# Expert value rows on TensorE as four 64x64 products, with no share for VectorE

## The chip, the cores and the metric

The kernel runs on one core of a Trainium2 chip. The metric is the device time of one execution in microseconds. Three executions of the kernel before took 3182.41, 3187.84 and 3185.2 us (median 3185.2 us).

## The reference, cut to what matters

The program is a transformer block with a mixture of convolution and RWKV, followed by a PEER feed-forward with 16384 experts, followed by two further layers (differential attention, then latent attention, each with a squared-ReLU MLP of width 4096). Everything is float32, with 512 tokens of width 1024. The change is in the PEER part, in its last line:

```python
def chunk(xc):                       # xc: 128 tokens x 1024
    q = (xc @ w_q).reshape(tc, 8, 2, 128)
    s = einsum('thpd,hpkd->thpk', q, sub_keys)
    ...                              # two rounds of top 16: expert and gate, 128 tokens x 8 heads x 16
    ue = take(expert_u, expert, axis=0)
    ve = take(expert_v, expert, axis=0)
    h = gelu(einsum('thkd,td->thk', ue, xc))
    return einsum('thk,thkd->td', gate * h, ve)
```

Each token picks 128 experts (8 heads times 16). For each of them a row of `expert_u` is multiplied with the token and a row of `expert_v` is added to the output with a weight of its own.

## The kernel before, in words

The 512 tokens are four tiles of 128, a token on each partition. A step, numbered n from 0 to 511, deals with expert number n % 128 of all tokens of tile n // 128. In a step:

- GpSimd (L1764, `pool_rows`) issues an indirect DMA that fetches one row of 2048 floats for each of 128 tokens: 1024 of u, then 1024 of v, 1 MB in all. The destinations are ten buffers, later six or seven (`row_of`); the profile's names for them are raw, w, un and scratch.
- VectorE (L1889, `dve_dot`) multiplies the u part with the tokens and sums over the row, which gives 128 numbers.
- ScalarE (L1838, L1840, L1845, `act_weight`) makes gelu, the product with the gate, and a diagonal 128x128 matrix with the weights on it.
- TensorE (L1783, `pe_rows`) multiplies the diagonal with the v part and adds up in two PSUM banks. Both operands are plain float32, and the trace shows each such product as two passes, each with a weight load of its own.

For n below 256 TensorE adds both column halves (two products of 128x128 with 128x512). From n = 256 on (`both_add`) TensorE adds the first 512 columns only and VectorE the other 512 with one scalar_tensor_tensor on PSUM (L1869). A row's buffer is refilled when whoever adds it has ticked `("acc", n)`: TensorE, and from 256 on VectorE too.

The order of the work on each engine is that of the Python generators. `with_rows` and `beside` lay the first 256 rows beside the choice of experts for the next token tiles, and the rows 256 to 511 between the pieces of the tail (`tail_gemm`, `pe_values`, `attention`, the MLPs) of the first half of the tokens (H.h = 0), 1.1 rows for each piece of weight 1. A weight tile of an MLP is a piece of weight 1, a step of an attention one of weight 1.2 (19 steps for each attention: 16 blocks and three to fill and empty the pipeline of scores L2297 to L2299, softmax, turn L2192 and product with the values L2206). After them comes the tail of the second half without any rows. In the tail all weight products have float32r operands: a weight tile is split into a high part (ScalarE, L296) and a low part (GpSimd, L302) and each product is three products (high x high, high x low, low x high), which the trace shows as three passes of 256 columns. One weight tile of the MLPs (L2544 up, L2563 down) is 24 such passes and comes as a DMA of 512 KB.

When 128 rows of a tile of tokens are added, ScalarE copies the two banks to `sums` (`act_join`), TensorE turns them over (`pe_join`) and VectorE adds them to the residual `xT` (`dve_join`).

Of the kernel before, what the change touches and what calls it, by code (L numbers as in the profile page):

```python
# [53 lines left out]
def shape_constants():  # L54
# [3 lines left out]
    same = (r // 64) == (c // 64)  # L58
    m = {"ident": r == c, "ones": np.ones((128, 128)), "bd": same, "iota": np.broadcast_to(c, (128, 128)),
         "causal": np.where(c <= r, 0.0, NEG), "strict": same & (r < c), "incl": same & (r <= c),  # L60
# [131 lines left out]
class Net:  # L192
# [1179 lines left out]
    def peer_tiles(self):  # L1372
# [35 lines left out]
        self.dots, self.gelus, self.weight = ([s[:, 128 * i:128 * i + 128] for s in small] for i in range(3))  # L1408
        self.diag = [[s[:, 512 + 128 * i:640 + 128 * i] for i in range(4)] for s in small]

# [12 lines left out]
    @staticmethod  # L1423
    def both_add(n):

        return n >= 256
# [312 lines left out]
    def pool_rows(self, e):  # L1739
# [3 lines left out]
        for n in range(512):  # L1743
# [7 lines left out]
            if before is not None:  # L1751
                e.wait_ge(*self.at("peer_pe", ("acc", before)))
                if self.both_add(before):
                    e.wait_ge(*self.at("peer_dve", ("acc", before)))
            elif r == 10:
                e.wait_ge(*self.at("peer_act", "xn moved"))
            elif r >= 6:
                e.wait_ge(*self.at("lo", ("peer_w_q", r - 2)))
            elif r < 4:
                e.wait_ge(*self.at("peer_pe", ("peer_w_q", 13 + 2 * (r // 2))))  # L1760
            else:
                e.wait_ge(*self.at("peer_pe", ("xn", 3, 1)))
# [9 lines left out]
    def pe_rows(self, e):  # L1772
        S, D_, A_ = "peer_pe", "peer_dve", "peer_act"
        for step in range(-1, 512 + LAG):
            n = self.late(step)
            if n is not None:
                tt, k = n // 128, n % 128
                b = 4 if tt == 0 else 6
                if k == 0 and tt >= 2:
                    e.wait_ge(*self.at(A_, ("sums", tt - 1)))  # L1780
                e.wait_ge(*self.at(A_, ("diag", n)))
                for half in range(1 if self.both_add(n) else 2):
                    ins = e.matmul(self.ps[:, b + half, :], self.diag[n >= 128][n % 4],  # L1783
                                   self.rows[self.row_of(n)][:, 1024 + 512 * half:1536 + 512 * half], start=k == 0,
                                   stop=k == 127)
                ins.then_inc(*self.tick(S, ("acc", n)))
                self.spot[("row", n)] = self.turn
# [4 lines left out]
    def pe_join(self, e, tt):  # L1792
# [3 lines left out]
        for half in range(2):  # L1796
            tile, freed = ("join", tt, half), ("join_dve", ("x", tt, 4 * half + 3))
            o, before = self.slot(tile, freed)
            for f in before:
                e.wait_ge(*self.at(*f))  # L1800
            for k in range(4):
                c = 512 * half + 128 * k
                ins = e.transpose(o[:, 128 * k:128 * k + 128], self.sums[tt % 2][:, c:c + 128], self.C("ident"))
            ins.then_inc(*self.tick(S, tile))
# [28 lines left out]
    def act_weight(self, e, n):  # L1833
# [8 lines left out]
        if n >= 4:  # L1842
            e.wait_ge(*self.at("peer_pe", ("acc", n - 4)))
        e.wait_ge(*self.at(S, ("weight", n)))
        e.activation(self.diag[n >= 128][n % 4], self.C("ident"), ACT.Identity, bias=0.0,  # L1845
                     scale=weight[:, c]).then_inc(*self.tick(S, ("diag", n)))

    def act_join(self, e, tt):
        b = 4 if tt == 0 else 6
        e.wait_ge(*self.at("peer_pe", ("acc", 128 * tt + 127)))  # L1850
        if tt >= 2:
            e.wait_ge(*self.at("peer_dve", ("acc", 128 * tt + 127)))
            e.wait_ge(*self.at("peer_pe", ("join", tt - 2, 1)))
        e.copy(self.sums[tt % 2], self.ps[:, b:b + 2, :].rearrange("p b n -> p (b n)")).then_inc(*self.tick("peer_act", ("sums", tt)))

    def dve_rows(self, e):
        S, A_, P_ = "peer_dve", "peer_act", "peer_pe"
        for n in range(-1, 512 + LAG):
            if n + 1 < 512:
                self.dve_dot(e, n + 1)  # L1860
            if 0 <= n < 512 and self.both_add(n):
                v, w, acc = self.rows[self.row_of(n)][:, 1536:2048], self.weight[1][:, n % 128:n % 128 + 1], self.ps[:, 7, :]
                e.wait_ge(*self.at(A_, ("weight", n)))
                if n % 128 == 0:
                    e.wait_ge(*self.at(A_, ("sums", n // 128 - 1)))
                    e.tensor_scalar(acc, v, w, None, ALU.mult).then_inc(*self.tick(S, ("acc", n)))
                else:
                    e.wait_ge(*self.at(S, ("acc", n - 1)))
                    e.scalar_tensor_tensor(out=acc, in0=v, scalar=w, in1=acc, op0=ALU.mult,  # L1869
                                           op1=ALU.add).then_inc(*self.tick(S, ("acc", n)))  # L1870
            if n in (130, 386 + LAG):
# [4 lines left out]
    def dve_dot(self, e, n):  # L1876
# [7 lines left out]
        xn = self.XN[:, n // 128, :]  # L1884
        if self.both_add(n):
            e.wait_ge(*self.at("peer_act", ("xn", n // 128)))
            xn = self.xn_bank()
# [5 lines left out]
    def dve_join(self, e, tt, j):  # L1893
        ts = slice(128 * tt, 128 * tt + 128)
        e.wait_ge(*self.at("peer_pe", ("join", tt, j // 4)))
        e.scalar_tensor_tensor(out=self.xT[:, j, ts], in0=self.bh(("join", tt, j // 4), 512)[:, 128 * (j % 4):128 * (j % 4) + 128],
                               scalar=self.modv[:, 40 + j:41 + j], in1=self.xT[:, j, ts], op0=ALU.mult,
                               op1=ALU.add).then_inc(*self.tick("join_dve", ("x", tt, j)))

# [1288 lines left out]
```

## Time and profile before

| | before |
|---|---|
| median of three executions | 3185.2 us (3182.41 to 3187.84) |
| the profiled execution, first to last instruction | 3185.9 us |
| instructions | 43155 |
| TensorE matmul busy | 2732.1 us (86%) |
| VectorE busy | 1985.9 us (62%) |
| ScalarE busy | 1445.6 us (45%) |
| GpSimd busy | 1682.5 us (53%) |
| rows 0 to 255 beside the choice of experts | about 742 to 1350 us |
| rows 256 to 511 beside the tail of the first half | about 1428 to 2445 us |

No time of the profiled execution is recorded beside its span, which lies within the spread of the three unprofiled ones. A pass that TensorE shows as 0.59 us long may be followed by the next after 0.43 us, since matmuls are pipelined; the distance from start to start is the occupancy, the duration is not. In the rows, PE is TensorE's matmuls, PEld its weight loads, DVE VectorE, ACT ScalarE, POOL GpSimd. A form such as 64*128 says how many rows and columns of the array an instruction uses.

### The profile page before, as it was taken

Reading aid. Unit: us, or ns where it says so; the run is one execution under the profiler, and the core shown is the slowest. Engines: PE = TensorE matmul, PEld = TensorE weight load, DVE = VectorE, ACT = ScalarE, POOL = GpSimd, SP = SyncE. Lnnn points to the kernel's source line nnn. Section 1 sums busy time; section 2 is a strip of 40 time slices with the busy share of each in tenths; the row PEclk is TensorE's granted clock in tenths of the full one; section 3 lists DMA queues with packets and bytes.
Section 4 is the critical chain, followed back from the end, with each engine's and each line's share of the span. In section 5 each row is a group of like instructions: output and inputs, shape, how many; then the busy total and the mean of one; then the engine's idle time right before and its main releaser. Section 6 shows DMA issues by size and latency. Waiting matters only on the chain.

```text
span 3185.9 us, 43155 instructions
## 1 busy us (share of the span) xinstructions
PE 2732.1 (86%) x15358; PEld 2107.2 (66%) x15358; DVE 1985.9 (62%) x4201; ACT 1445.6 (45%) x3202; POOL 1682.5 (53%) x1014
## 2 busy tenths in 40 slices
PE   6986997798877877769889998769997999999998
PEld 3855897575333333228557786547876979998998
DVE  5676444465777777767677667767667364246323
ACT  2232222223344434345776555686555355444553
POOL 4813222273444444347437886528884607863685
PEclk8988998799999999989889999989998999999999
DMA  7220001127999999988969998889997505542453
GB/s 288 95 77 1 1 1 53 80 93 302 421 421 422 421 421 421 387 321 315 378 257 360 404 414 350 327 305 367 410 407 287 165 27 153 191 151 82 142 177 119
DMA packets 140516, 797.46 MB, mean 250 GB/s; under 512 B 15504, under 2 KB 18704, under 8 KB 67600
## 3 DMA queue, kind: packets, MB, share of 16 engines
q0 software_dynamic: 73728, 536.90, 41.5%
q1 hardware_dynamic: 65856, 253.36, 22.5%
q10 hardware_dynamic: 720, 4.46, 0.3%
q8 instruction: 123, 2.02, 0.2%
q14 instruction: 89, 0.73, 0.1%
HBM read 788.10 MB, written 6.55 MB: 249 GB/s over the span
## 4 chain that ended last, share of the span: by engine, by line
PE 43%; DVE 14%; DMA 14%; POOL 9%; issue 8%; ACT 6%; DVEq 0%; ACTq 0%; SPq 0%; POOLq 0%
PE ps L2544 7%; PE ps L2563 7%; PE ps L879 6%; PE ps L1783 6%; PE ps L1989 6%; DMA raw<-in_peer_uv,un 5%; POOL wls L302 4%; DVE scratch L1889 3%; PE ps L332 3%; POOL wlw L302 2%; DMA un<-in_peer_uv,un 2%; DMA w<-in_peer_uv,scratch 2%; DMA raw<-in_peer_uv,scratch 1%; DMA w<-in_peer_uv,un 1%; POOL raw L1764 1%
## 5 line engine op out<-in xcount | busy, mean ns | idle before, releaser
L302 POOL TENSOR_TENSOR wls<-raws,whs 128x1024 fp32r<-128x1024 f32 (+1 forms) x256 | 612.1, 2400 | 375.7 <-ACT whs L296 368.0
L1783 PE MATMUL ps<-raw,un 128*128 128x512 f32 x522 | 275.0, 637 | 65.9 <-ACT un L1845 61.6
L1989 PE MATMUL ps<-ts,whs 128*128 128x256 f32 x1424 | 302.2, 313 | 30.9 <-DVE ts L2084 19.7
L1764 POOL DMA_INDIRECT raw<-in_peer_uv,un x205 | 205.8, 1004 | 200.8 <-PE ps L1783 124.9
L296 ACT CAST whs<-raws 128x1024 fp32r<-128x1024 f32 (+1 forms) x256 | 263.8, 1036 | 94.7 <-PE ps L2563 35.2
L302 POOL TENSOR_TENSOR wlw<-raws,whw 128x1024 fp32r<-128x1024 f32 x112 | 267.9, 2405 | 71.6 <-ACT whw L296 71.0
L1989 PEld LDWEIGHTS ps<-ts,whs 128*128 128x128 f32 x1424 | 240.4, 203 | 62.8 <-issue 32.8
L1838 ACT ACTIVATE un<-un 128x1 f32<-128x1 f32 x384 | 77.6, 202 | 432.9 <-DVE scratch L1889 423.7
L2563 PE MATMUL ps<-ts,whs 128*128 128x256 f32 x1216 | 239.6, 298 | 1.5 <-DVE ts L2616 1.5
L1889 DVE SCALAR_TENSOR_TENSOR scratch<-raw,ps 128x1024 f32<-128x1024 f32 x149 | 181.3, 1217 | 87.0 <-DMA raw<-in_peer_uv,un 82.7
L2544 PE MATMUL ps<-ts,whs 128*128 128x256 f32 x1088 | 209.9, 294 | 0.0
L1989 PE MATMUL ps<-ts,wls 128*128 128x256 f32 x712 | 208.5, 293 | 0.0
L2563 PEld LDWEIGHTS ps<-ts,whs 128*128 128x128 f32 x1216 | 192.2, 191 | 23.4 <-issue 21.4
L302 POOL TENSOR_TENSOR wl<-raw,wh 128x2048 fp32r<-128x2048 f32 x23 | 106.9, 4651 | 172.2 <-ACT wh L296 172.2
L2544 PE MATMUL ps<-ts,whw 128*128 128x256 f32 x960 | 189.1, 298 | 9.6 <-DVE ts L2084 9.6
L1783 PEld LDWEIGHTS ps<-raw,un 128*128 128x128 f32 x522 | 93.1, 202 | 146.8 <-ACT un L1845 98.1
L1783 PE MATMUL ps<-un 128*128 128x512 f32 x268 | 146.5, 654 | 41.9 <-ACT un L1845 36.5
L2544 PEld LDWEIGHTS ps<-ts,whs 128*128 128x128 f32 x1088 | 171.4, 191 | 14.9 <-issue 14.0
L2645 DVE TENSOR_TENSOR kept<-kept,ps 128x256 f32<-128x256 f32 x256 | 103.2, 417 | 115.1 <-PE ps L2563 115.0
L2563 PE MATMUL ps<-ts,wls 128*128 128x256 f32 x608 | 171.7, 282 | 0.0
L1845 ACT ACTIVATE un<-kept,un 128x128 f32<-128x128 f32 x384 | 154.4, 402 | 36.1 <-ACT un L1840 0.7
L2544 PEld LDWEIGHTS ps<-ts,whw 128*128 128x128 f32 x960 | 153.0, 193 | 24.8 <-issue 13.3
(453 smaller groups left out, 7388.7 us busy)
## 6 DMA issues: line engine op xcount, KB each, us to landing
raws<-in_w_up SPq DMA_DIRECT2D x128, 512.0 KB
raws<-in_w_down SPq DMA_DIRECT2D x128, 512.0 KB
scratch<-in_ada_w SPq DMA_DIRECT2D x17, 1024.0 KB, 13.0
raws<-in_w_qk SPq DMA_DIRECT2D x32, 512.0 KB
raw<-in_w_in SPq DMA_DIRECT2D x11, 1024.0 KB, 5.9
raw<-in_peer_w_q SPq DMA_DIRECT2D x8, 1024.0 KB, 8.1
raws<-in_w_v SPq DMA_DIRECT2D x16, 512.0 KB
raws<-in_w_o_a SPq DMA_DIRECT2D x16, 512.0 KB
```

The source lines that it names most:

```text
L296: e.copy(self.wh[h][:, 0:width], self.raw[slot][:, 0:width]).then_inc(*self.tick("hi", key))
L302: e.tensor_tensor(self.wl[h][:, 0:width], self.raw[slot][:, 0:width], self.wh[h][:, 0:width].bitcast(F32), ALU.subtract).then_inc(*self.ti ...
L332: ins = e.matmul(self.ps[:, b, :], l, r, start=k == 0 and i == 0, stop=k == nk - 1 and i == 2)
L879: ins = e.matmul(self.ps[:, b, 128 * q:128 * q + 128], l, r, start=n == 0, stop=n == len(terms) - 1)
L1764: e.indirect_dma_start(self.rows[r], None, self.d["peer_uv"], index).then_inc(*self.tick(f"row{r}", n, 16))
L1783: ins = e.matmul(self.ps[:, b + half, :], self.diag[n >= 128][n % 4], self.rows[self.row_of(n)][:, 1024 + 512 * half:1536 + 512 * half], s ...
L1845: e.activation(self.diag[n >= 128][n % 4], self.C("ident"), ACT.Identity, bias=0.0, scale=weight[:, c]).then_inc(*self.tick(S, ("diag", n)))
L1889: e.scalar_tensor_tensor(out=self.junk[0 if n < 128 else n % 2 if n < 256 else 1], in0=self.rows[r][:, 0:1024], scalar=1.0, in1=xn, op0=AL ...
L1989: ins = e.matmul(o[:, 0:256], l, r, start=k == 0 and i == 0, stop=k == nk - 1 and i == 2)
L2544: ins = e.matmul(o[:, 0:256], l, r, start=k == 0 and n == 0, stop=k == 7 and n == 2)
L2563: ins = e.matmul(o[:, 0:256], l, r, start=t == 0 and n == 0, stop=t == 3 and n == 2)
L2645: e.tensor_tensor(x, x, self.bh((P_, "v", g, j)), ALU.add).then_inc(*self.tick(S, ("x", g, j)))
```

## The change

Every value row, for all n, is added by TensorE alone. The two or one products with a 128x128 diagonal become four products for each row: partitions 0 to 63 and 64 to 127 of the row (hd) times column halves 0 and 1 (half). The stationary operand is 64x64, so the four products lie on the four quadrants of the array: the input partitions p select the rows of the array, and the output partitions o its columns. The output of row group hd goes to bank b + hd, partitions 64*half to 64*half + 63. ScalarE writes a 128x64 tile, two diagonals of 64 one above the other, in place of a 128x128 one. The constant that was "iota" keeps its first 64 columns and holds these diagonals in the other 64. VectorE's additions (L1869) and all waits for them are gone. The sums now lie otherwise in PSUM, so the joins pick other columns; their number and sizes stay, but one VectorE operation reads two pieces of 64 columns.

```diff
-        self.diag = [[s[:, 512 + 128 * i:640 + 128 * i] for i in range(4)] for s in small]
+        self.diag = [[s[:, 512 + 64 * i:576 + 64 * i] for i in range(4)] for s in small]
+        self.each64 = self.C("iota")[:, 64:128]
...
@@ pool_rows
             if before is not None:
                 e.wait_ge(*self.at("peer_pe", ("acc", before)))
-                if self.both_add(before):
-                    e.wait_ge(*self.at("peer_dve", ("acc", before)))
...
@@ pe_rows
-                for half in range(1 if self.both_add(n) else 2):
-                    ins = e.matmul(self.ps[:, b + half, :], self.diag[n >= 128][n % 4],
-                                   self.rows[self.row_of(n)][:, 1024 + 512 * half:1536 + 512 * half], start=k == 0,
-                                   stop=k == 127)
+                row, diag = self.rows[self.row_of(n)], self.diag[n >= 128][n % 4]
+                for half in range(2):
+                    for hd in range(2):
+                        p, o = slice(64 * hd, 64 * hd + 64), slice(64 * half, 64 * half + 64)
+                        ins = e.matmul(self.ps[o, b + hd, :], diag[p, :], row[p, 1024 + 512 * half:1536 + 512 * half],
+                                       start=k == 0, stop=k == 127)
                 ins.then_inc(*self.tick(S, ("acc", n)))
...
@@ pe_join
-                c = 512 * half + 128 * k
+                c = 512 * (k % 2) + 128 * (2 * half + k // 2)
...
@@ act_weight
-        e.activation(self.diag[n >= 128][n % 4], self.C("ident"), ACT.Identity, bias=0.0,
+        e.activation(self.diag[n >= 128][n % 4], self.each64, ACT.Identity, bias=0.0,
                      scale=weight[:, c]).then_inc(*self.tick(S, ("diag", n)))
...
@@ dve_rows
-            if 0 <= n < 512 and self.both_add(n):
-                v, w, acc = self.rows[self.row_of(n)][:, 1536:2048], self.weight[1][:, n % 128:n % 128 + 1], self.ps[:, 7, :]
-                e.wait_ge(*self.at(A_, ("weight", n)))
...
-                    e.wait_ge(*self.at(S, ("acc", n - 1)))
-                    e.scalar_tensor_tensor(out=acc, in0=v, scalar=w, in1=acc, op0=ALU.mult,
-                                           op1=ALU.add).then_inc(*self.tick(S, ("acc", n)))
```

How the rows stand among the MLP's passes on TensorE, in the first MLP of the first half (L2544 is the up product; ts is the activation, whs, whw, wls and wlw are the parts of the weights, un and raw are row buffers and diagonals). Before:

```order
L2544 MATMUL ps<-ts_89,wls_82 128x256
L1783 MATMUL ps<-un 128x512
L2544 MATMUL ps<-ts_89,whw_83 128x256 x2
L2544 MATMUL ps<-ts_89,wlw_84 128x256
L2544 MATMUL ps<-ts_89,whw_83 128x256 x2
```

After the change the same place (the up product is now line 2535):

```order
L2535 MATMUL ps<-ts_89,wls_82 128x256
L1785 MATMUL ps<-un 64x512 x4
L2535 MATMUL ps<-ts_89,whw_83 128x256 x2
L2535 MATMUL ps<-ts_89,wlw_84 128x256
L2535 MATMUL ps<-ts_89,whw_83 128x256 x2
```

One product over the full array has become four with 64 rows each, and full-array products stand ahead of and behind them as before. Nothing else on TensorE has another place.

On TensorE, too, among the first 256 rows, a place where two rows follow each other (L1516 and L1517 turn over the normed activations, uh and ul). Before:

```order
L1516 MATMUL ps<-kept,uh 128x128
L1517 MATMUL ps<-kept,ul 128x128
L1783 MATMUL ps<-raw_65,scratch 128x512 x2
L1783 MATMUL ps<-raw_66,scratch 128x512 x2
L1516 MATMUL ps<-kept,uh 128x128
```

After:

```order
L1517 MATMUL ps<-kept,uh 128x128
L1518 MATMUL ps<-kept,ul 128x128
L1785 MATMUL ps<-raw_65,scratch 64x512 x4
L1785 MATMUL ps<-raw_66,scratch 64x512 x4
L1517 MATMUL ps<-kept,uh 128x128
```

The two products of a row are four, and rows follow each other or the choice of experts.

On VectorE, in an MLP of the first half (L1889 is the dot product of a row, L2645 the addition to the residual), before:

```order
L2645 TENSOR_TENSOR kept<-kept,ps 128x256
L1889 SCALAR_TENSOR_TENSOR scratch,un<-raw_64,ps 128x1024
L1869 SCALAR_TENSOR_TENSOR ps<-un,ps 128x512
L2645 TENSOR_TENSOR kept<-kept,ps 128x256
L1889 SCALAR_TENSOR_TENSOR scratch,un<-raw_65,ps 128x1024
L1869 SCALAR_TENSOR_TENSOR ps<-raw_64,un,ps 128x512
```

and after:

```order
L2636 TENSOR_TENSOR kept<-kept,ps 128x256
L1879 SCALAR_TENSOR_TENSOR scratch,un<-raw_64,ps 128x1024
L2636 TENSOR_TENSOR kept<-kept,ps 128x256
L1879 SCALAR_TENSOR_TENSOR scratch,un<-raw_65,ps 128x1024
L2636 TENSOR_TENSOR kept<-kept,ps 128x256 x2
```

Each addition of L1869 behind a dot product is gone, and what stood behind it moves up.

## Rows read from the trace of the kernel before

**Rows 1.** The page: the span, and part 1, busy time of each engine.

```profile
span 3185.9 us, 43155 instructions
PE 2732.1 (86%) x15358; PEld 2107.2 (66%) x15358; DVE 1985.9 (62%) x4201; ACT 1445.6 (45%) x3202; POOL 1682.5 (53%) x1014
```

**Rows 2.** Busy time of each engine in stretches, (x) instructions, clock, DMA.

```profile
core 0: us, PE busy (x) PEld busy (x) DVE busy (x) ACT busy (x) POOL busy (x), PEclk, DMA share, GB/s
742.00:1350.00 608.00, 482.26 (x1120) 202.93 (x1120) 455.40 (x1223) 237.83 (x742) 265.15 (x234) 0.94 0.98 407
1428.00:1507.00 79.00, 74.44 (x467) 64.45 (x468) 55.81 (x118) 40.49 (x88) 52.55 (x31) 0.93 0.80 310
1538.00:1640.00 102.00, 80.35 (x257) 42.11 (x257) 81.42 (x227) 89.76 (x220) 30.56 (x31) 0.82 0.85 323
1700.00:1900.00 200.00, 192.28 (x1302) 164.21 (x1301) 133.38 (x259) 112.10 (x266) 165.25 (x102) 1.00 0.98 395
2046.00:2140.00 94.00, 61.20 (x212) 37.12 (x211) 60.13 (x148) 76.69 (x166) 29.54 (x28) 0.85 0.86 326
2200.00:2400.00 200.00, 192.26 (x1306) 163.83 (x1305) 135.38 (x264) 112.43 (x264) 167.29 (x104) 1.00 1.01 408
```

**Rows 3.** The same view, instructions of L1783 (value rows) alone.

```profile
742.00:1350.00 608.00, 463.93 (x944) 181.27 (x944) 0.94 0.98 407
1428.00:1507.00 79.00, 18.16 (x34) 6.62 (x34) 0.93 0.80 310
1700.00:1900.00 200.00, 56.75 (x110) 17.19 (x110) 1.00 0.98 395
2200.00:2400.00 200.00, 57.07 (x110) 17.06 (x110) 1.00 1.01 408
1428.00:2445.00 1017.00, 281.56 (x508) 86.13 (x508) 0.94 0.90 355
```

**Rows 4.** Timeline of TensorE among the first 256 rows (start, duration, instruction).

```profile
899.77 6.60 PE L1783 MATMUL ps<-raw,scratch 128*128 128x512 f32 x15
```

**Rows 5.** Timeline of TensorE in an MLP, one weight tile's first and last passes.

```profile
1904.49 0.40 PE L2544 MATMUL ps<-ts,whs 128*128 128x256 f32 x2
...
1907.25 0.28 PE L2544 MATMUL ps<-ts,wls 128*128 128x256 f32 x1
1907.37 0.59 PE L1783 MATMUL ps<-un 128*128 128x512 f32 x1
```

**Rows 6.** Timeline of TensorE, L690: products of 64 rows, alternating partitions 0-63, 64-127.

```profile
184.63 2.08 PE L690 MATMUL ps<-scratch 64*128 64x512 f32 x8 [3.79 <-DVE ps L630]
```

**Rows 7.** Timeline of TensorE: 64-row products beside 128-row ones, in an attention.

```profile
2601.49 0.59 PE L2298 MATMUL ps<-k,q 64*128 64x256 f32 x2
2602.01 0.30 PEld L2299 LDWEIGHTS ps<-kept 128*128 128x128 f32 x2 [0.33 <-issue]
2603.22 0.39 PE L2206 MATMUL ps<-at,v 128*128 128x128 f32 x2
2603.54 0.29 PEld L2297 LDWEIGHTS ps<-ka,q 64*128 64x128 f32 x2
```

**Rows 8.** Groups, 1428 to 2445 us: count | busy, mean ns | idle before, releaser.

```profile
L1869 DVE SCALAR_TENSOR_TENSOR ps<-raw,un,ps 128x512 f32<-128x512 f32 x146 | 109.7, 751 | 1.3 <-ACT un L1840 1.2
L1840 ACT ACTIVATE un<-un 128x1 f32<-128x1 f32 x252 | 74.3, 295 | 8.2
L1845 ACT ACTIVATE un<-kept,un 128x128 f32<-128x128 f32 x253 | 101.8, 402 | 23.4
```

**Rows 9.** Chain that ended last, by line: 1538 to 1640, then 2046 to 2140 us.

```profile
by line: ACT L2378 16.4%; ACT L1838 15.1%; DMA raw<-in_peer_uv,un 15.0%; issue 14.3%; ACT e L2378 8.7%; ACT un L1840 4.8%; DVE ps L1869 4.7%; ACT un L1838 3.0%; ACT at L2197 2.7%; ACT un L1845 2.6%; ACT q L2391 2.5%; POOL wls L302 2.3%; PE 
by line: issue 29.8%; DVE scratch L1889 12.8%; DMA raw<-in_peer_uv,un 12.5%; DVE ps L1869 12.2%; ACT me L2814 7.1%; ACT L2814 5.2%; DVE kept L2926 3.7%; ACT mat L2197 3.2%; ACT ts L2824 2.6%; POOL wls L302 2.5%; DVE kept L2928 2.0%; ACT un 
```

More of the change, by code:

```diff
@@ L58, in shape_constants @@
     same = (r // 64) == (c // 64)
-    m = {"ident": r == c, "ones": np.ones((128, 128)), "bd": same, "iota": np.broadcast_to(c, (128, 128)),
+    m = {"ident": r == c, "ones": np.ones((128, 128)), "bd": same, "iota": np.where(c < 64, c, r % 64 == c % 64),
          "causal": np.where(c <= r, 0.0, NEG), "strict": same & (r < c), "incl": same & (r <= c),
@@ L1423, in both_add, with xn_in_psum @@
     @staticmethod
-    def both_add(n):
+    def xn_in_psum(n):
         return n >= 256
@@ L1796, in pe_join @@
         for half in range(2):
-            tile, freed = ("join", tt, half), ("join_dve", ("x", tt, 4 * half + 3))
+            tile, freed = ("join", tt, half), ("join_dve", ("x", tt, 5 + 2 * half))
             o, before = self.slot(tile, freed)
@@ L1851, in act_join @@
         if tt >= 2:
-            e.wait_ge(*self.at("peer_dve", ("acc", 128 * tt + 127)))
             e.wait_ge(*self.at("peer_pe", ("join", tt - 2, 1)))
@@ L1860, in dve_rows @@
                 self.dve_dot(e, n + 1)
-            if 0 <= n < 512 and self.both_add(n):
-                v, w, acc = self.rows[self.row_of(n)][:, 1536:2048], self.weight[1][:, n % 128:n % 128 + 1], self.ps[:, 7, :]
-                e.wait_ge(*self.at(A_, ("weight", n)))
[L1864 to L1867, printed above, removed]
-                    e.wait_ge(*self.at(S, ("acc", n - 1)))
-                    e.scalar_tensor_tensor(out=acc, in0=v, scalar=w, in1=acc, op0=ALU.mult,
-                                           op1=ALU.add).then_inc(*self.tick(S, ("acc", n)))
             if n in (130, 386 + LAG):
@@ L1884, in dve_dot @@
         xn = self.XN[:, n // 128, :]
-        if self.both_add(n):
+        if self.xn_in_psum(n):
             e.wait_ge(*self.at("peer_act", ("xn", n // 128)))
@@ L1893, in dve_join @@
     def dve_join(self, e, tt, j):
[L1894 to L1898, printed above, removed]
+        tile = ("join", tt, j % 4 // 2)
+        x = self.xT[:, j, 128 * tt:128 * tt + 128].rearrange("p (s n) -> p s n", n=64)
+        turned = self.bh(tile, 512).rearrange("p (k s d n) -> p k s d n", s=2, d=2, n=64)
+        e.wait_ge(*self.at("peer_pe", tile))
+        e.scalar_tensor_tensor(out=x, in0=turned[:, j % 2, :, j // 4, :], scalar=self.modv[:, 40 + j:41 + j], in1=x,
+                               op0=ALU.mult, op1=ALU.add).then_inc(*self.tick("join_dve", ("x", tt, j)))
     def tail_tiles(self):
```

## The prediction

> **What bounds the kernel now.** The page comes first: TensorE is busy for 86% of the span, but its durations overlap, and VectorE, which loses work here, is at 62% [rows 1]. An average over stages decides nothing, so I read the busy time by stretches next [rows 2], once with all instructions and once with those of the value rows alone [rows 3]. Four kinds of stretch come out.
>
> First, rows 0 to 255 (742 to 1350 us): the DMA share is 0.98, the mean rate 407 GB/s [rows 2]. A row is 1.05 MB, so 608 us hold what the transfers can carry: 944 passes of L1783, four for each row, are 236 rows there [rows 3], 2.58 us for each. TensorE needs four passes at the pitch of [rows 4]: 15 passes last 6.60 us, the last of them 0.59, so (6.60 - 0.59) / 14 = 0.43 us from start to start and 1.72 us for a row. It waits for transfers.
>
> Second, the MLPs of the first half (1700 to 1900 and 2200 to 2400 are clean pieces of them). There the passes that aren't of rows are 1302 - 110 + 1306 - 110 = 2388, which at 24 for each weight tile are 99.5 tiles in 400 us, 4.02 us for each, with 110 rows (two passes for each), 1.1 for each tile [rows 2, 3]. TensorE's need: a tile's 24 passes start at 1904.49 and the next product at 1907.37, so 2.88 us [rows 5], and 1.1 x 0.86 for rows, 3.83 us in all. The DMA share is 0.98 and 1.01 [rows 2]. So transfers bound the MLPs, and TensorE is only 0.19 us of each tile behind them. This is the place that decides.
>
> Third, the projections (1428 to 1507, for one): 467 passes of which 34 are of rows [rows 2, 3], that is 433 x 0.12 + 34 x 0.43 = 67 us of TensorE's need in 79.
>
> Fourth, the two attentions. TensorE shows 61 of 94 us in the second one and 80 of 102 in the first, ScalarE 77 and 90 [rows 2]. The chain runs through ScalarE, DMA landings and VectorE; the addition L1869 holds 4.7% of it in the first (4.8 us) and 12.2% in the second (11.5 us) [rows 9].
>
> After 2445 us there are no value rows and nothing changes.
>
> **The change part by part.**
>
> *VectorE's additions go.* 252 or so of them at 751 ns [rows 8], 191 us of VectorE's time over 256 rows. In the MLPs VectorE is at 133 and 135 of 200 us [rows 2] and isn't the bound, so this is worth nothing there. In the attentions the chain gives 4.8 + 11.5 = 16 us, less what other waits take over. For projections and joints I add 10 us, an estimate between nothing and the attentions' share. In all -26 us; bounds 0 and -50.
>
> *ScalarE's diagonal is half as wide.* One column costs 295 ns and 128 columns 402 [rows 8], so 64 should cost 0.35: -0.05 us for each row, 50 rows in attentions, -2.5 us. I leave it in the bound above.
>
> *TensorE's products.* Each row now has eight passes of 64 rows by 64 columns, each with 512 moving columns. What they cost depends on how many run side by side. Nothing in this trace splits the array by columns. It does split it by rows: L690 multiplies partitions 0 to 63 and 64 to 127 in turn. Eight passes take 2.08 us from the first start to the last end [rows 6], so the last starts 1.49 us after the first; one after another they would need 7 x 0.43 = 3.0. In pairs they need 3 x 0.43 = 1.29, and 0.20 is left for the first weight load and a stagger of some 0.13 between the tiles. So the two row groups do run side by side, both passes of each. For the columns there are two ends: four side by side, 0.86 us plus three staggers of 64-column loads (I take half of 0.13, so 0.19), 1.05 us for a row; or only the two row groups side by side, 4 x 0.43 + 0.13 = 1.85 us. I take the first, since the quadrants have separate outputs and the split by rows has shown itself free of loss.
>
> *Two changes of the array's split for each row.* Between 64-row and 128-row products the trace shows a gap. The second pass of L2298 starts 0.21 us after 2601.49 and feeds 256 columns for 0.21, until 2601.92, but the next weight load starts at 2602.01 and its first data 0.11 later, as the two loads of a pair are 0.11 apart: 0.20 us lost. In the other direction the two passes of L2206 from 2603.22 feed until 2603.44, the load starts at 2603.54, the data at 2603.65: 0.21 us lost [rows 7]. Before the change a row stood among the MLP's passes without any gap, 0.12 us behind the last of them [rows 5]. Now each row alone among full-array products pays both ways, 0.41 us; a 64-column load may save 0.05 of it, so 0.35. The bounds are 0 (the gap belongs to plain float32 alone, or hides) and 0.45.
>
> The Trainium skill's "TensorEngine Tiling (Array Packing)", section Key Properties, speaks against this change: changing the tiling mode, as against the tile, drains TensorE. The trace agrees, with the 0.20 and 0.21 us above. By this rule a row in the MLPs costs 1.40 us; by its neighbour in the same list, that tiles work independently, alone, 1.05.
>
> *Sum for the MLPs.* A row costs 1.05 + 0.35 = 1.40 us in place of 0.86, a tile 2.88 + 1.1 x 1.40 = 4.42 us. That is above the 4.02 that transfers set, so TensorE becomes the bound and the time of a tile rises by 0.40 us. The two MLPs of the first half have 128 tiles; I count 120, as the ends are ragged: +48 us.
>
> *Sum for the rest.* The projections hold what is left of the 256 rows, 256 - 141 in MLPs - 50 in attentions (38 steps of 1.3 rows), 65; 65 x 0.54 = 35 us more of TensorE's need, of which at 67 of 79 us some 40% is felt: +14. In the attentions 50 x 0.54 = 27 us, a quarter felt: +7. Rows 0 to 255: eight passes at 1.05 us, at most 1.85, stay below 2.58, so the transfers hide all of it: 0. Should TensorE's clock fall there for lack of work (it is granted 0.94 now [rows 2]), 1.05 at half the clock is 2.1 us, still covered. If that cover were gone, it would cost the difference over 236 rows.
>
> *The row buffers.* GpSimd now waits for TensorE alone. In MLPs with TensorE as the bound the buffers come free at TensorE's pace, and what is late next is the refill, which has 0.4 us of slack for each tile. Nothing more.
>
> Total: +48 + 14 + 7 - 26 = +43 us on the profiled execution's 3185.9, so 3229; it stands 0.7 us above the median of the three, so 3228 us.
>
> **The rivals.**
>
> *Faster: the gap for the split doesn't show in these places.* Then a row costs 1.05 us and a tile 2.88 + 1.16 = 4.04, level with the transfers' 4.02, and the -26 us remain with some +5 for projections: about 3165 us. For it: the gap in [rows 7] is seen only between plain float32 products, and weight loads for four quadrants might be taken ahead. It decides below a row cost of about 1.15 us. Against: both directions show it alike. Chance 27%, with a stronger relief of VectorE inside it.
>
> *The parts cancel* within 0.2%: 5%.
>
> *Three slots.* If the passes of a row group queue in order, the first column tile's second pass runs beside the second one's first: 3 x 0.43 + 0.1 + 0.35 = 1.74 us, tile 4.79, 0.77 x 120 = +92, others +36, -26: about 3287 us. Chance 9%.
>
> *Rows only.* The columns aren't split in time: 1.85 + 0.35 = 2.20 us, tile 5.30, +154 in MLPs, 65 x 1.34 x 0.7 = +61 in projections, +20 in attentions, -26: about 3395 us. For it: nothing in the trace splits columns. Chance 10%. A strict order of all passes would come out close to it: eight passes of which only those at a border between tiles overlap need five slots, 2.15 us. The Trainium skill's "TensorE: Matmul & The Clock Gate", section Part 3 (the mechanism), says that matmuls start and end strictly in program order; by it the estimate is the five slots. The trace disagrees for row groups: L690's last start at 1.49 us fits three slots, not the four of that order (1.71).
>
> *All one after another*: 3.43 us for a row, above the 2.58 of the transfers even in the first stage; over 3700 us. [rows 6] speaks against it. Chance 3%.
>
> **How the numbers follow.** My forecast has 46%, with 3195 to 3262 as its own range (a row between 1.2 and 1.6 us). Slower holds 46 + 9 + 10 + 3 = 68%, less a little for forecasts that end near zero: 0.66; faster 0.28; same 0.06. A change of this kernel can be told from none at about 0.2%, 6 us. The range from 3150 to 3300 takes in the faster rival, the forecast and the three slots, and leaves out the last two with 13% and some tails.
>
> **What the changed profile would show.** The row line's eight passes in the MLPs span about 1.05 us from the first start to where the last stops feeding, and the distance from the last MLP pass ahead to the first behind is 1.4 us more than without a row. In the same MLP stretches tiles pass at 4.4 us and the DMA share falls to about 0.9. The first 256 rows keep their 608 us. The attentions get shorter by 10 to 20 us together. It would be wrong if passes overlap less, if no gap shows at the changes, or if the attentions, by VectorE's relief, give back more than 40 us.

## The result, and the profile after

Six executions of the changed kernel took 3197.82 us in the median (3185.76 to 3203.47), six of the kernel before 3184.78 us (3182.41 to 3188.53). The ratio is 1.0039 (95% interval 1.0024 to 1.0054): 13 us slower. The profiled execution has a span of 3199.6 us, 13.7 more than that of before.

The page of the changed kernel, its span and part 1, against [rows 1]:

```profile
span 3199.6 us, 47517 instructions
PE 2674.9 (84%) x17918; PEld 1954.9 (61%) x17918; DVE 1832.2 (57%) x3945; ACT 1418.2 (44%) x3202; POOL 1681.6 (53%) x1014
```

VectorE has lost 154 us of busy time and 256 instructions, and the span has grown. (The 256 additions add up to some 190 us, but an engine's neighbouring instructions overlap in part, and the page counts overlapping time once.) TensorE's busy time, too, is less than before although there are 2560 more passes: passes that run side by side are counted once.

The stretches of [rows 2], in the changed kernel:

```profile
core 0: us, PE busy (x) PEld busy (x) DVE busy (x) ACT busy (x) POOL busy (x), PEclk, DMA share, GB/s
742.00:1350.00 608.00, 370.84 (x2072) 93.21 (x2074) 458.05 (x1227) 227.13 (x747) 267.58 (x235) 0.74 0.98 408
1428.00:1507.00 79.00, 74.73 (x546) 54.94 (x539) 46.88 (x101) 37.08 (x85) 54.25 (x32) 0.96 0.81 299
1538.00:1640.00 102.00, 86.01 (x442) 41.89 (x441) 66.24 (x200) 89.00 (x221) 30.49 (x31) 0.82 0.85 326
1700.00:1900.00 200.00, 200.00 (x1563) 151.12 (x1563) 99.09 (x202) 108.16 (x263) 161.66 (x100) 1.00 0.97 386
2200.00:2400.00 200.00, 200.00 (x1567) 151.68 (x1567) 98.84 (x202) 105.20 (x255) 160.75 (x99) 1.00 0.99 393
```

and those of [rows 3], the value rows alone (L1785 now; eight passes for each row):

```profile
742.00:1350.00 608.00, 347.42 (x1900) 70.81 (x1904) 0.74 0.98 408
1700.00:1900.00 200.00, 57.02 (x424) 11.30 (x424) 1.00 0.97 386
2200.00:2400.00 200.00, 56.17 (x416) 11.01 (x416) 1.00 0.99 393
```

In the MLP stretches TensorE is busy for 200.00 of 200 us, where it was for 192. Its passes that are not of rows are 1563 - 424 + 1567 - 416 = 2290, which is 95.4 weight tiles in 400 us: 4.19 us for a tile, against 4.02. In the first stage 1900 passes are 237 rows in 608 us, as many as before, and the transfers still run at 0.98; the granted clock has fallen from 0.94 to 0.74 there, and it cost nothing (first_only below).

The chain that ended last is the sequence of instructions and waits, followed back from the end, that set the time. Between 1700 and 1900 us, by line, it holds TensorE alone in the changed kernel. L2535, L2554 and L1785 are the MLP's products and the rows:

```profile
by line: PE ps L2535 41.2%; PE ps L2554 32.1%; PE ps L1785 26.8%
```

The timeline of TensorE there, to compare with [rows 5]: one row between two weight tiles.

```profile
1803.62 0.28 PE L2554 MATMUL ps<-ts,wls 128*128 128x256 f32 x1
1803.83 1.09 PE L1785 MATMUL ps<-un 64*64 64x512 f32 x8
1804.85 0.51 PE L2554 MATMUL ps<-ts,whs 128*128 128x256 f32 x2
```

and of its weight loads:

```profile
1803.83 0.21 PEld L1785 LDWEIGHTS ps<-un 64*64 64x64 f32 x8
1804.85 0.30 PEld L2554 LDWEIGHTS ps<-ts,whs 128*128 128x128 f32 x2 [0.81 <-issue]
```

Narrow windows of the same timeline (1803.70 to 1803.832, 1803.91 to 1804.30 and 1804.50 to 1804.80 us) take the row's merged line apart, into its first pass, its first four and its last four:

```profile
1803.83 0.64 PE L1785 MATMUL ps<-un 64*64 64x512 f32 x1
1803.83 0.66 PE L1785 MATMUL ps<-un 64*64 64x512 f32 x4
1804.31 0.61 PE L1785 MATMUL ps<-un 64*64 64x512 f32 x4
```

A single pass without a wait shows 0.59 us [rows 5]. The first one has 0.05 more, which is the weight load that it waits for; four passes together have 0.02 more than one, which is the whole stagger of the four. So four passes run side by side, then four more, 0.43 us behind the first data at 1803.88. The four quadrants do work side by side.

The MLP's last pass feeds until 1803.62 + 0.12 = 1803.74. The next MLP pass has its load at 1804.85 and its first data 0.11 later, at 1804.96. So a row takes 1.22 us of TensorE's time. It is made up of 0.09 until the row's first load starts, 0.05 of that load, 0.86 for the two passes of each quadrant, 0.02 of stagger, 0.09 until the MLP's next load starts, and 0.11 of that load. The parts that are not passes come to 0.36: that is the price of going to the quadrants and back.

Where the 13.7 us of the profiled executions come from, by the starts of TensorE's first and last passes of each stage in the traces (us; the last columns belong to experiments below; w_qk, w_v, w_o_a and w_o_b are projections too):

| stretch of the first half | before | changed | dve_back | full | threes | pairs_order |
|---|---|---|---|---|---|---|
| w_qk and w_v | 109.6 | 116.5 | 117.9 | 128.6 | 112.3 | 112.2 |
| first attention | 97.7 | 94.7 | 96.5 | 91.5 | 102.3 | 98.1 |
| w_o_a | 53.6 | 54.9 | 58.1 | 57.9 | 60.8 | 55.0 |
| first MLP | 271.1 | 279.0 | 272.8 | 310.8 | 271.0 | 273.2 |
| projections of the latent attention | 86.3 | 84.9 | 87.4 | 87.9 | 94.2 | 85.7 |
| its scores | 81.7 | 79.2 | 85.3 | 76.2 | 76.4 | 76.5 |
| w_o_b | 53.4 | 53.0 | 55.3 | 56.3 | 62.8 | 53.9 |
| second MLP | 256.4 | 269.3 | 271.0 | 304.1 | 259.1 | 259.8 |

The two MLPs give +20.8, the two attentions -5.5, the projections together +6.4. The first stage ends 5.5 us earlier, about 2 of it before the first value row; such shifts ahead of any changed instruction are over 7 us between profiled executions of these kernels (the first value row stands at 742.4 before, 740.2 in the changed kernel and 734.8 in pairs_order), so small differences of spans are not read. The rest, -2.4, lies after the last row. Each column is one execution. The first MLP shows how much that matters: it takes 279.0 us here, 274.6 in second_only and 272.8 in dve_back, whose rows cost TensorE the same. The two MLPs' +20.8 is +16 in both of those.

### The profile page after: what moved, and what is told of

The parts are those of the page before. It is cut to its first block, busy times and chain, and to the rows that moved or that the text cites. A ratio compares the mean times of both kernels' runs of the same rounds, so it can differ in the third digit from the quotient of the medians.

```text
span 3199.6 us, 47517 instructions
## 1 busy us (share of the span) xinstructions
PE 2674.9 (84%) x17918; PEld 1954.9 (61%) x17918; DVE 1832.2 (57%) x3945; ACT 1418.2 (44%) x3202; POOL 1681.6 (53%) x1014
## 4 chain that ended last, share of the span: by engine, by line
PE 55%; DMA 15%; DVE 12%; ACT 6%; issue 3%; POOL 3%; ACTq 0%; DVEq 0%; SPq 0%; POOLq 0%
PE ps L2554 12%; PE ps L2535 11%; PE ps L1785 8%; PE ps L879 6%; PE ps L1980 6%; DMA raw<-in_peer_uv,un 4%; DMA w<-in_peer_uv,scratch 4%; PE ps L332 3%; DMA un<-in_peer_uv,un 3%; DVE scratch L1879 2%; DMA un<-in_peer_uv,scratch 2%; POOL wls L302 1%; DMA w<-in_peer_uv,un 1%; PE ps L2221 1%; DMA raw<-in_peer_uv,scratch 1%
## 5 line engine op out<-in xcount | busy, mean ns | idle before, releaser
L302 POOL TENSOR_TENSOR wls<-raws,whs 128x1024 fp32r<-128x1024 f32 (+1 forms) x256 | 612.4, 2402 | 392.4 <-ACT whs L296 390.1
L1785 PE MATMUL ps<-raw,un 64*64 64x512 f32 x1640 | 252.8, 699 | 83.2 <-ACT un L1846 81.0
L302 POOL TENSOR_TENSOR wlw<-raws,whw 128x1024 fp32r<-128x1024 f32 x112 | 267.5, 2403 | 79.6 <-ACT whw L296 78.6
L1980 PE MATMUL ps<-ts,whs 128*128 128x256 f32 x1424 | 286.3, 302 | 24.4 <-DVE ts L2075 18.2
L1980 PEld LDWEIGHTS ps<-ts,whs 128*128 128x128 f32 x1424 | 234.5, 201 | 70.4 <-issue 42.7
L2554 PE MATMUL ps<-ts,whs 128*128 128x256 f32 x1216 | 226.7, 287 | 0.0
L2554 PEld LDWEIGHTS ps<-ts,whs 128*128 128x128 f32 x1216 | 189.4, 192 | 36.6 <-issue 18.7
L2600 DVE SCALAR_TENSOR_TENSOR ps<-ps,rs 128x256 f32<-128x256 f32 x128 | 55.4, 433 | 260.1 <-PE ps L2535 245.6
L2535 PE MATMUL ps<-ts,whs 128*128 128x256 f32 x1088 | 201.0, 286 | 0.0
L302 POOL TENSOR_TENSOR wl<-raw,wh 128x2048 fp32r<-128x2048 f32 x23 | 106.8, 4649 | 172.1 <-ACT wh L296 172.1
L2535 PE MATMUL ps<-ts,whw 128*128 128x256 f32 x960 | 181.8, 290 | 11.0 <-DVE ts L2075 11.0
L2535 PEld LDWEIGHTS ps<-ts,whs 128*128 128x128 f32 x1088 | 169.3, 192 | 25.2 <-issue 13.8
L2535 PEld LDWEIGHTS ps<-ts,whw 128*128 128x128 f32 x960 | 151.6, 194 | 35.5 <-issue 16.2
L2554 PE MATMUL ps<-ts,wls 128*128 128x256 f32 x608 | 172.1, 283 | 0.0
L1879 DVE SCALAR_TENSOR_TENSOR scratch<-raw,scratch 128x1024 f32<-128x1024 f32 x108 | 135.7, 1262 | 52.0 <-DMA raw<-in_peer_uv,un 28.8
L1785 PE MATMUL ps<-un 64*64 64x512 f32 x832 | 131.6, 713 | 38.0 <-ACT un L1846 35.6
```

The lines of the kernel that those rows point to most:

```text
L302: e.tensor_tensor(self.wl[h][:, 0:width], self.raw[slot][:, 0:width], self.wh[h][:, 0:width].bitcast(F32), ALU.subtract).then_inc(*self.ti ...
L1785: ins = e.matmul(self.ps[o, b + hd, :], diag[p, :], row[p, 1024 + 512 * half:1536 + 512 * half], start=k == 0, stop=k == 127)
L1879: e.scalar_tensor_tensor(out=self.junk[0 if n < 128 else n % 2 if n < 256 else 1], in0=self.rows[r][:, 0:1024], scalar=1.0, in1=xn, op0=AL ...
L1980: ins = e.matmul(o[:, 0:256], l, r, start=k == 0 and i == 0, stop=k == nk - 1 and i == 2)
L2535: ins = e.matmul(o[:, 0:256], l, r, start=k == 0 and n == 0, stop=k == 7 and n == 2)
L2554: ins = e.matmul(o[:, 0:256], l, r, start=t == 0 and n == 0, stop=t == 3 and n == 2)
```

## The experiments

Each ratio below is against executions of the kernel before that were taken beside the run; their medians are 3183.0, 3183.2 and 3182.5 us.

Theory A: in the two MLPs of the first half TensorE's need for a tile, 2.88 us + 1.1 times the cost of a row, went above the transfers' 4.0 us, and that is the loss. Rival B: a colder clock of TensorE in the first stage. Rival C: not TensorE's time but the release of row buffers, which now waits for TensorE alone. Beside them, the size of VectorE's relief was open.

**first_only** and **second_only**: the change on one side of row 256 only. `quarters(n)` is n < 256 or n >= 256. The heart of the edit, which also brings back the other side's diagonals, additions and joins (left out here):

```diff
-                for half in range(2):
+                for half in range(0 if self.quarters(n) else 1 if self.both_add(n) else 2):
+                    ins = e.matmul(self.ps[:, b + half, :], diag, row[:, 1024 + 512 * half:1536 + 512 * half], start=k == 0,
+                                   stop=k == 127)
+                for half in range(2 if self.quarters(n) else 0):
...
```

> Four 64x64 products only for rows 0 to 255; rows 256 to 511 as before (TensorE the left 512 columns, VectorE the right). Theory A (TensorE's need in the MLPs of the first half sets the loss, 0.36 us more for each row there): nothing of the loss is left, since these rows stand under the transfers; the first stage ends about 4 us earlier as in the changed kernel: 3181 us (3176 to 3185). Rival B (the loss is a colder TensorE clock, 0.74 in place of 0.94 in the first stage, that is carried on): slower than before, 3190 or more.

> The complement: rows 0 to 255 with full products as before, rows 256 to 511 as four 64x64 products and nothing on VectorE. Theory A: the whole loss and a little more, 3202 us (3197 to 3207); MLP stretches of the first half at 4.2 us for a weight tile. Rival B: 3185 or less.

Measured: first_only 3185.39 us, ratio 1.0001 (0.9987 to 1.0015); second_only 3198.01 us, ratio 1.0038 (1.0024 to 1.0052). The whole loss is on the side of the rows from 256 on. Rival B falls: first_only has the cold clock (0.74 granted from 742 to 1350 us) and no loss. The first stage gains nothing that can be measured either, where I had expected 4 us. second_only's weight tiles pass at 4.21 us in the two MLP stretches, by the same counting of passes, and its time is the expected one.

**dve_back**: the changed kernel, with VectorE's additions back as work that nobody uses. The row buffers wait for VectorE again, too.

```diff
...
+            if 256 <= n < 512:
+                v, w, out = self.rows[self.row_of(n)][:, 1536:2048], self.weight[1][:, n % 128:n % 128 + 1], self.junk[1][:, 0:512]
...
+                e.scalar_tensor_tensor(out=out, in0=v, scalar=w, in1=self.xn_bank()[:, 0:512], op0=ALU.mult,
+                                       op1=ALU.add).then_inc(*self.tick(S, ("again", n)))
```

> The changed kernel, and VectorE makes its 256 additions of 512 columns again, into a scratch that nobody reads; the row buffers wait for both again. Theory A with a small relief: the relief of VectorE was worth 5 to 10 us, all of it outside the MLPs: 3198 + 8 = 3206 us. As the prediction had it (relief 26 us): 3224. If the relief is worth nothing: 3198.

Measured: 3208.23 us, ratio 1.0069 (1.0056 to 1.0082), 10 us above the changed kernel, as expected with a small relief. So the relief of VectorE is worth 10 us, not 26; by the two intervals an estimate of its error is 6 us. The line of these additions shows the same price for one as L1869 had [rows 8], so the work was really put back:

```profile
L1871 DVE SCALAR_TENSOR_TENSOR scratch<-raw,un,ps 128x512 f32<-128x512 f32 x145 | 108.4, 748 | 14.7 <-ACT un L1845 0.8
```

Against dve_back the changed kernel's attentions are 7.9 us shorter together and the projections 9.4, the MLPs 4.5 longer, in these single executions. The prediction had 16, 10 and nothing. In the scores alone the additions are worth 6.1 us (85.3 against 79.2), where the chain had 11.5 on L1869 [rows 9]. Why less than the chain promised is seen in the changed kernel's chain of the second attention, 2052 to 2146 us:

```profile
by line: DVE scratch L1879 22.8%; ACT L2805 17.7%; DMA raw<-in_peer_uv,un 14.2%; issue 9.9%; POOL wls L302 7.5%; ACT me L2805 7.1%; ACT un L1841 4.5%; ACT mat L2188 3.3%; PE ps L1785 3.2%; ACT un L1839 3.2%; ACT ts L2815 2.3%; PE ps L2197 1
```

L1869's 12.2% are gone. The dot product (12.8% before, 22.8% now) and ScalarE (L2805, 25% with its table loads, against 12%) have taken over most of the place. Against the kernel before the scores gain only 2.5 us, since their rows cost TensorE more now.

**full**: the kernel before with both halves as full products on TensorE.

```diff
...
-                for half in range(1 if self.both_add(n) else 2):
+                for half in range(2):
...
```

> The kernel before with TensorE adding both halves as full 128x128 products for all rows, nothing on VectorE. A row costs TensorE 1.72 us and no change of the split. Theory A: a weight tile of the MLPs takes 2.88 + 1.1 x 1.72 = 4.77 us against 4.02 before, +94 us for the two MLPs, about +28 in projections, +10 in attentions, -8 relief: 3185 + 124 = 3309 us (3280 to 3330). Rival C (TensorE's time isn't what matters, the release of row buffers is): below 3250.

Measured: 3281.59 us, ratio 1.0304 (1.0289 to 1.0320). In two MLP stretches, all instructions and then the rows alone (L1781, four passes each):

```profile
1760.00:1960.00 200.00, 200.00 (x1194) 155.66 (x1193) 85.56 (x175) 94.76 (x223) 144.57 (x89) 1.00 0.92 352
2300.00:2500.00 200.00, 200.00 (x1191) 155.30 (x1190) 87.14 (x178) 95.42 (x227) 145.31 (x90) 1.00 0.93 354
```

```profile
1760.00:1960.00 200.00, 86.38 (x185) 32.16 (x186) 1.00 0.92 352
2300.00:2500.00 200.00, 87.15 (x187) 31.86 (x185) 1.00 0.93 354
```

(1194 - 185 + 1191 - 187) / 24 = 83.9 tiles in 400 us, 4.77 us for a tile: the number that theory A gave. The two MLPs cost +87 us, where 94 were expected. The time is 27 us below the expectation. By the table the projections cost the +28 that were put down, but the attentions got 12 us shorter, where +10 for them less 8 of relief were put down; the rest, some 7 us, lies outside the stages of the table and isn't explained. Without the quadrants, then, taking VectorE off costs 97 us; with them 13.

**pairs**: two rows' products together, from row 256 on, so that the split changes twice for two rows.

```diff
-            if n is not None:
+            group = () if n is None else (n,) if n < 256 else range(n - 1, n + 1) if n % 2 == 1 else ()
+            for n in group:
                 tt, k = n // 128, n % 128
```

> The changed kernel, but from row 256 on TensorE does a row's four products together with those of the next row, so that the array's split changes twice for two rows. Nothing else moves. Theory A: a row costs 0.86 + 0.18 = 1.04 us, a tile of the MLPs 2.88 + 1.1 x 1.04 = 4.02 us, level with the transfers: 3198 - 20 = 3178 us (3170 to 3186). Rival C (what costs is that row buffers come free later): 3200 or more, since every other row is held longer.

**threes** and **fours**: larger groups, with eight diagonals. Here, other than in pairs, the place of a row that orders GpSimd's queue (`spot`) stays at the step in which the changed kernel adds it:

```diff
             if n is not None:
+                self.spot[("row", n)] = self.turn
+            group = () if n is None else (n,) if n < 256 else range(n - (n % 128) % 3, n + 1) if (n % 128) % 3 == 2 or n % 128 == 127 else ()
+            for n in group:
...
-                self.spot[("row", n)] = self.turn
```

> As pairs, in groups of three rows, with eight diagonals in place of four. Theory A: a row costs 0.86 + 0.12 = 0.98 us, a tile 3.96, below the transfers, so little more than pairs: 3176 us. Rival C: slower than pairs and than before, as a group holds three of six or seven buffers.

> As threes, in groups of four rows. TensorE's need falls to 2.88 + 1.1 x 0.95 = 3.93 us for a tile. Theory A alone: 3176 us; with the buffers as the next limit (a group of four holds more than half of the seven): 3190 or more. Rival C: far slower, 3230.

Measured: pairs 3232.03 us, ratio 1.0147 (1.0125 to 1.0169); threes 3203.73 us, 1.0061 (1.0042 to 1.0079); fours 3220.09 us, 1.0117 (1.0096 to 1.0138). None is what theory A alone gave (3178, 3176 and 3176); pairs falls where rival C had put it, and fours where the buffers as the next limit had put it. threes is slower than the kernel before, but not slower than pairs as rival C wanted: the smallest group is the slowest. By stages (table above) threes brings the MLPs back to 271.0 and 259.1 us, which is 18 us less than the changed kernel, and loses that and more outside them (first attention +8, w_o_a +6, the latent attention's projections +9, w_o_b +10). The waits speak for row buffers as the limit there. The first two lines of GpSimd's waits for TensorE's rows in threes, 1980 to 2180 us (total, times, longest):

```profile
POOL raw L1763 <- PE ps L1788: 54.3, 13, 11.9
...
POOL un L1763 <- PE ps L1788: 33.2, 7, 14.5
```

and in the changed kernel in the same stretch:

```profile
POOL raw L1763 <- PE ps L1785: 34.5, 12, 7.0
...
POOL un L1763 <- PE ps L1785: 19.7, 7, 5.4
```

So rival C holds where groups are large, outside the MLPs, and doesn't explain the changed kernel's loss. Two runs put the groups where theory A wants them, and one asks what made pairs slow.

**mlp_threes**, **mlp_pairs**: groups for the rows of the two MLPs alone. **pairs_order**: pairs with the order line of threes, nothing else. In mlp_threes, `in_mlp(n)` is 322 <= n < 390 or n >= 441:

```diff
...
+            group = () if n is None else (n,) if not self.in_mlp(n) else range(n - n % 128 % 3, n + 1) if n % 128 % 3 == 2 or n % 128 == 127 else ()
...
```

> Groups of three rows as in threes, but only for the rows that fall into the two MLPs of the first half (322 to 389 and 441 to 511); all other rows one at a time as in the changed kernel, with eight diagonals. Theory A: in threes the MLPs took 271 and 259 us against 279 and 269 of the changed kernel, and the attentions and projections lost what that won, since groups hold row buffers where rows come late. With the groups in the MLPs alone the 18 us are kept: 3198 - 18 = 3180 us (3174 to 3188). If groups cost in buffers in the MLPs too: 3195 or more.

> As mlp_threes in groups of two (rows 320 to 389 and 442 to 511). Theory A: a row 1.04 us, a tile 4.02, level with the transfers: 3182 us (3176 to 3190).

> Groups of two everywhere from row 256 on and four diagonals, as pairs, but GpSimd's queue keeps the order it has in the changed kernel (in pairs the fetches of rows came to stand behind weight splits, since the code orders them by where TensorE is done with a row). If that order made pairs slow: between 3185 and 3205 us, like threes. If the four diagonals did: 3225 to 3235 again.

Measured: mlp_threes 3178.95 us, ratio 0.9993 (0.9983 to 1.0002); mlp_pairs 3179.25 us, 0.9996 (0.9984 to 1.0009); pairs_order 3175.84 us, 0.9977 (0.9964 to 0.9990). All three take back the loss, the first two as theory A said (3180, 3182). pairs_order is faster than both kernels. Its expectation, 3185 to 3205, was too high: I had expected groups of two to cost something outside the MLPs as threes does, and the table shows next to nothing of that; the 3178 that theory A gave for pairs is what it came to. The MLPs take 266.3 and 258.2 us in mlp_threes, 270.2 and 259.6 in mlp_pairs, so the gain is where theory A puts it. The eight diagonals are no cause of what threes loses outside the MLPs either: mlp_threes has them, and takes 51.9, 85.4 and 53.0 us where threes takes 60.8, 94.2 and 62.8.

pairs_order's timeline of TensorE in the first MLP: two rows, one change in and one out.

```profile
1802.88 0.28 PE L2537 MATMUL ps<-ts,wlw 128*128 128x256 f32 x1
1803.09 1.95 PE L1788 MATMUL ps<-raw,un 64*64 64x512 f32 x16
1804.97 0.51 PE L2537 MATMUL ps<-ts,whw 128*128 128x256 f32 x2
```

From 1802.88 + 0.12 to 1804.97 + 0.11 are 2.08 us, 1.04 for a row: four times 0.43 for two rows, and 0.36 once. The MLP stretches of pairs_order, all and the rows alone (L1788):

```profile
1700.00:1900.00 200.00, 198.43 (x1618) 157.52 (x1611) 100.16 (x207) 107.13 (x262) 162.41 (x101) 1.00 1.00 399
2200.00:2400.00 200.00, 199.70 (x1632) 158.96 (x1631) 100.54 (x207) 106.75 (x258) 167.54 (x103) 1.00 1.01 407
```

```profile
1700.00:1900.00 200.00, 52.55 (x428) 13.21 (x420) 1.00 1.00 399
2200.00:2400.00 200.00, 52.81 (x432) 13.77 (x432) 1.00 1.01 407
```

(1618 - 428 + 1632 - 432) / 24 = 99.6 tiles in 400 us: 4.02 us for a tile, and the DMA share is back at 1.00 and 1.01. TensorE's need and the transfers meet there.

The table holds a second test of theory A. w_qk and w_v have 26 rows, and the stretch takes 109.6 us before and 108.6 in first_only, whose rows there are as before. With single rows of quadrants it takes 116.5 to 117.9 us (changed, second_only, dve_back, mlp_threes, mlp_pairs), with groups 112.2 and 112.3 (pairs_order, threes), with full products 128.6. Only pairs (116.7, with its other order of GpSimd's queue) and fours (119.4, with its large groups) stand apart. The added need of TensorE is 26 x 0.36 = 9.4, 26 x 0.18 = 4.7 and 26 x 0.86 = 22.4 us, and the added time (about 7 to 8, 3 and 19) follows it in the same order. So this stage, too, has TensorE close to its bound.

Pairs and pairs_order differ in GpSimd's queue alone, and by 56 us. In pairs the code took a row to be done later and put weight splits (L302) ahead of the fetches of rows: in the two traces up to four more splits stand before a fetch in pairs, while pairs_order has the changed kernel's order throughout. The waits of VectorE's dot product for landings, 1700 to 1900 us, in pairs:

```profile
DVE scratch L1880 <- DMA raw<-in_peer_uv,un: 52.8, 24, 5.4
DVE scratch L1880 <- DMA un<-in_peer_uv,un: 27.6, 14, 4.2
```

and in pairs_order:

```profile
DVE scratch L1881 <- DMA raw<-in_peer_uv,un: 39.1, 23, 4.8
...
DVE scratch L1881 <- DMA un<-in_peer_uv,un: 16.7, 10, 2.8
```

## Why the prediction was wrong in size

The direction, the place and the mechanism were right: TensorE became the bound in the MLPs of the first half, and the change of the split did it. second_only, full, mlp_pairs and pairs_order show it. The forecast of +43 us was more than three times the measured 13. By its steps:

- *TensorE's products.* This is the term that was mis-sized. The step took 1.05 us for a row: 0.86 and 0.19 of stagger, the latter three times half of L690's 0.13. Measured are 0.86 and 0.02 of stagger for all four quadrants. That the quadrants run side by side, which nothing in the trace before showed for columns, is now shown. Halving L690's stagger had no ground but the half width of the load.
- *Two changes of the split.* Taken at 0.35, measured at 0.34 without the stagger: 0.09 and 0.05 on the way in, 0.09 and 0.11 on the way out. Both directions of [rows 7] were the right price. The Trainium skill's "TensorEngine Tiling (Array Packing)", section Key Properties, says that a change of the mode drains TensorE. The trace agrees: on either side of a row 0.09 us pass in which TensorE starts neither a load nor a pass.
- *Sum for the MLPs.* This is the step that failed by it: a row of 1.22 us in place of 1.40 gives 2.88 + 1.34 = 4.22 us for a tile (measured 4.19) in place of 4.42. As 4.02 was the floor in any case, an error of 0.18 in 1.40 halved the excess: +21 us in place of +48, and only +16 in second_only and dve_back. The model is borne out by four points: 4.77 worked out and measured (full), 4.22 and 4.19 (changed), 4.02 and 4.02 (pairs_order, where need and transfers can't be told apart), and before, with a need of 3.83, the transfers' 4.02.
- *The rest of TensorE's need.* +14 for projections and +7 for attentions. dve_back against before has VectorE's additions on both sides and shows these terms by themselves: +15.8 in projections, +2.4 in attentions. The felt shares were guesses; the one for projections came out right, the one for attentions was too high.
- *VectorE's additions.* -26 us in the prediction, -10 by dve_back. Reading a line's share of the chain as its worth was the error: the two attentions were to give 16 us and gave 7.9, as the dot product and ScalarE stood close behind. This error made the forecast lower and hid a part of the other.
- *ScalarE's diagonal* at 0.35 us: right, 348 ns.
- *Rows 0 to 255* at nothing: right, by first_only; with the colder clock (0.74), as the step allowed for.
- *The row buffers.* "Nothing more" was right for the changed kernel, and threes shows how near that limit is outside the MLPs.

Of the signs that the prediction named, the gap at the changes came, with 1.22 us for a row in place of 1.4. Tiles pass at 4.19 us in place of 4.4, and the DMA share is 0.97 and 0.99, not 0.9. The attentions got 5.5 us shorter, not 10 to 20.

The rivals "three slots", "rows only" and "all one after another" are ruled out by the row's timeline. The strict order of passes that stands beside them was put down as five slots; the row takes two. The faster rival was wrong about the gap, but pairs_order shows its other half: with a row at 1.04 us the change pays, by 0.2% (3175.84 us).

Open: why the execution profiled for the changed kernel has some 5 us more in its first MLP than second_only and dve_back have, and what makes up the few us outside the stages of the table.

## What to carry to other kernels

Where two limits lie close together (4.02 and 3.83 us here), work out each one's need for the unit of work and compare; a small error in the price of the nearer one is a large error in the excess. Splitting the array into quadrants made this diagonal product cost half (0.86 in place of 1.72 us for both halves of a row), but each trip to the quadrants and back cost 0.36 us. So such products should stand in groups, as large as the buffers they hold allow; here groups of two were enough, and groups of three and four lost more outside the MLPs than they won. A share of the chain is not what a removal brings: here it promised twice what came in the attentions, since other work stood close behind.

## What the runs showed of the hardware

- Four plain float32 products of 64x64 with 512 columns, with other moving data for each column half, run side by side: eight passes in 1.09 us from the first start to the last end, with 0.02 us of stagger over the four quadrants. One after another they would need 7 x 0.43 + 0.59 = 3.6 us, an estimate from the same pitch.
- All four quadrants' first passes start within 0.02 us, then all four second passes. The Trainium skill's "TensorE: Matmul & The Clock Gate", section Part 3 (the mechanism), says that matmuls start in program order. If the two passes of a float32 product stand together in that order, four quadrants need four times 0.43 us until the last start, 1.7 us; the trace shows 0.50. No run tells in which order the passes are issued, so this does not show that the order is broken, and the same holds for what the prediction says of L690.
- Going from full products to quadrants and back costs 0.36 us, and two rows that stand together pay it once: 2.08 us for two (pairs_order), 1.22 us for one.
- The granted clock in the first stage was 0.94 with TensorE busy for 482 of 608 us (1.72 us of row passes for each 2.6 us), and 0.74 with 371 us (0.86 for each row): a mean between its two levels, lower where TensorE was idle for longer between rows. It cost nothing (first_only), since transfers set the pace.
- The order of one queue (GpSimd's fetches against its splits) was worth 56 us (pairs against pairs_order), four times the change itself.
